# Extra expert blocks in pairs or one by one: the order of the blocks at the end of a mixture-of-experts loop

## The reference

```python
def hier_moe(h, rg_w, rg_b, re_w, re_b, w_gate, w_up, w_down):
    ...
    grp = jnp.argmax(g_logits, axis=-1)
    ...
    top_v, top_i = lax.top_k(e_sel, TOP_K_INNER)
    ...
    for g in range(N_GROUPS):
        hid = jax.nn.silu(jnp.einsum('td,edf->tef', t, w_gate[g])) * jnp.einsum('td,edf->tef', t, w_up[g])
        y = y + jnp.einsum('tef,efd->td', hid * combine[:, g, :, None], w_down[g])
```

## Time and profile before

| what | value |
|---|---|
| median of 3 runs | 718.06 us (713.32 to 723.28) |
| the profiled execution: its own time | 719.2 us |
| the profiled execution: span from first to last instruction | 717.4 us |
| mean granted clock of TensorE in it | 0.917 of full speed |
| PE busy | 585.8 us (82%) |
| DVE, ACT, POOL busy | 332.9, 143.7, 113.4 us |
| DMA moved | 180.99 MB, mean 252 GB/s |

### The profile page before, as it was taken

One profiled execution on the slowest core, in us unless ns is written; L12 is line 12 of the kernel. 1 busy time (PEld: TensorE's weight loads), 2 busy tenths in 40 slices (PEclk: granted clock), 3 DMA queues, 4 the chain that ended last, 5 costly groups with the idle time before them and its releaser, 6 DMA issues.

```text
span 717.4 us, 10963 instructions
## 1 busy us (share of the span) xinstructions
PE 585.8 (82%) x4542; PEld 366.9 (51%) x4542; DVE 332.9 (46%) x600; ACT 143.7 (20%) x371; POOL 113.4 (16%) x150
## 2 busy tenths in 40 slices
PE   3779999899987678999836999897877877769791
PEld 2459999676764365444524555443433444435320
DVE  2463442555642663496686244433333333343355
ACT  1441441254332153011111100000000000000132
POOL 4000000100001013000021232322222222221213
PEclk9769999999998599999965999999999999999887
DMA  8991311002006989901399799999999999998072
GB/s 302 370 248 60 69 62 56 16 1 91 27 1 220 375 306 273 311 30 60 109 407 364 288 413 410 411 409 408 409 413 411 410 408 406 408 401 313 31 266 117
DMA packets 71289, 180.99 MB, mean 252 GB/s; under 512 B 22164, under 2 KB 26108, under 8 KB 66628
## 3 DMA queue, kind: packets, MB, share of 16 engines
q1 hardware_dynamic: 60612, 163.39, 60.9%
q0 software_dynamic: 7936, 14.09, 5.6%
q10 hardware_dynamic: 2688, 2.77, 1.1%
HBM read 176.25 MB, written 14.45 MB: 266 GB/s over the span
## 4 chain that ended last, share of the span: by engine, by line
PE 44%; SPq 28%; DVE 11%; DMA 9%; ACT 4%; issue 3%; ACTq 0%; DVEq 0%; POOLq 0%
SPq L438 27%; PE bank L973 8%; PE bank L1219 8%; PE bank L1040 6%; PE bank L1323 5%; DMA ring<-in_ada_w_dram 3%; DMA ring<-in_moe_w_up_dram 3%; PE bank L1341 2%; PE bank L927 2%; PE bank L1022 2%; DMA x_tok<-in_x_sample_dram 2%; PE bank L1064 1%; PE bank L1081 1%; DVE x_tok L1912 1%; PE bank L1382 1%
## 5 line engine op out<-in xcount | busy, mean ns | idle before, releaser
L1323 PE MATMUL bank<-late_w,xT 128*64 128x256 f32 x672 | 83.4, 401 | 22.7 <-DMA late_w<-in_moe_w_up_dram 19.8
L1844 DVE COPY xT<-bank 128x512 f32<-128x512 f32 x38 | 26.2, 692 | 125.0 <-PE bank L1309 124.5
L1323 PE MATMUL bank<-ring,xT 128*64 128x256 f32 x480 | 64.8, 427 | 21.0 <-DMA ring<-in_moe_w_up_dram 19.0
L1323 PEld LDWEIGHTS bank<-late_w,xT 128*64 128x64 f32 x672 | 50.0, 139 | 62.2 <-DMA late_w<-in_moe_w_up_dram 30.5
L1323 PEld LDWEIGHTS bank<-ring,xT 128*64 128x64 f32 x480 | 37.4, 149 | 52.6 <-DMA ring<-in_moe_w_up_dram 28.5
L862 ACT ACTIVATE sgl<-bank 128x128 f32<-128x128 f32 x36 | 10.0, 278 | 249.3 <-PE bank L1323 249.3
L614 POOL DMA_INDIRECT expert_rows<-ye,dsti x36 | 36.6, 1016 | 128.2 <-DVE ye L1863 124.8
L607 POOL DMA_INDIRECT xg<-h_scratch,srci x38 | 39.0, 1026 | 102.6 <-PE bank L1309 92.7
L1860 DVE SCALAR_TENSOR_TENSOR S<-bank,modrt,S 128x512 f32<-128x512 f32 x36 | 27.0, 750 | 32.6 <-PE bank L1341 32.3
L1341 PE MATMUL bank<-late_w,hT 128*64 128x512 f32 x168 | 40.7, 604 | 0.0
L1040 PE MATMUL bank<-ring_r,h_high 128*128 128x512 f32 (+1 forms) x140 | 38.1, 412 | 0.0
(11 more groups left out here) (329 smaller groups left out, 858.1 us busy)
## 6 DMA issues: line engine op xcount, KB each, us to landing
ring<-in_ada_w_dram SPq DMA_DIRECT2D x22, 1024.0 KB, 11.3
late_w<-in_moe_w_gate_dram SPq DMA_DIRECT2D x21, 1024.0 KB, 16.9
late_w<-in_moe_w_up_dram SPq DMA_DIRECT2D x21, 1024.0 KB, 22.4
late_w<-in_moe_w_down_dram SPq DMA_DIRECT2D x21, 1024.0 KB, 22.4
ring<-in_moe_w_down_dram SPq DMA_DIRECT2D x15, 1024.0 KB, 22.7
ring<-in_moe_w_gate_dram SPq DMA_DIRECT2D x15, 1024.0 KB, 16.6
ring<-in_moe_w_up_dram SPq DMA_DIRECT2D x15, 1024.0 KB, 22.5
ring<-in_w_in_dram SPq DMA_DIRECT2D x7, 1024.0 KB, 5.6
```

The source lines that it names most:

```text
L1323: mm = pe.matmul(bank[2 + a][f * C:(f + 1) * C, 0:2 * P], x, w[:, kk, f, :, :], start=(kk == 0), stop=(kk == KD - 1))
L1844: dve.tensor_copy(xT[:, a, :, :], bank[a][:, :].rearrange("p (k n) -> p k n", k=4)).then_inc(xe_ev, 1)
```

## The change

It touches only the extra blocks and the last two steps of the static loop.

1. PE and DVE turn and copy the rows of blocks 32 and 33 inside the static loop, in the steps of experts 31 and 32 (the condition `e + 1 < E` goes). Before, both were turned behind the last `down` of the static loop, and copied behind its last `gated_rows`.
2. Inside a pair, PE, ACT, DVE and POOL finish the first block before they begin the second. Before, each kind of step was done for both blocks in turn.

```diff
@@ POOL
                         if b + 2 < NBLK:
                             pool.wait_ge(pe_xe, b + 1)
                             gather(b + 2, b % 2)
-                    for b in (E + 2 * i, E + 2 * i + 1):
                         scatter(b, b % 2)
@@ PE
-                if e + 1 < E:
-                    turn_x((e + 1) % 2, 16 * ((e + 1) // 2 + 1), e if e >= 1 else None)
+                turn_x((e + 1) % 2, 16 * ((e + 1) // 2 + 1), e if e >= 1 else None)
...
-            for b in (E, E + 1):
-                turn_x(b % 2, 16 * (b // 2 + 1), b - 1)
             pe.wait_ge(xe_ev, E + 2)
...
                         gate_up(b % 2, b % R, 32 * (b // R + 1), b + 1, b - 1)
-                    for b in (E + 2 * i, E + 2 * i + 1):
                         turn_h(b % 2, b + 1, b)
                         if b + 2 < NBLK:
                             turn_x(b % 2, 16 * ((b + 2) // 2 + 1), b + 1)
@@ DVE
-                if e + 1 < E:
-                    evac_x((e + 1) % 2, e + 2, gate_up_done(e - 1) if e >= 1 else None)
+                evac_x((e + 1) % 2, e + 2, gate_up_done(e - 1) if e >= 1 else None)
...
-            for b in (E, E + 1):
-                evac_x(b % 2, b + 1, gate_up_done(b - 2))
...
                         hidden(b % 2, b + 1, b - 1)
-                    for b in (E + 2 * i + 2, E + 2 * i + 3):
-                        if b < NBLK:
-                            evac_x(b % 2, b + 1, gate_up_done(b - 2))
-                    for b in (E + 2 * i, E + 2 * i + 1):
+                        if b + 2 < NBLK:
+                            evac_x(b % 2, b + 3, gate_up_done(b))
                         gated_rows(b, 16 * (b // 2))
```

## The result

The changed kernel took 733.95 us (median of 6 runs, 728.11 to 737.28) against 717.25 us for the kernel before (6 runs): a ratio of 1.0251, 95% interval 1.0212 to 1.0290, so 15 to 21 us slower. 733 was predicted, within 726 to 741.

The account below looks back on a forecast made before the run. Bound before: SP's weight loads, plus 10.7 us behind the last up matrix. Waits for gathers in the extra blocks add 14.8 us to the profiled 719.2, making 734.0; that profile lay 1.1 above the median, so 733 us, range 726 to 741.

Parts of the forecast that it names:

- The ring: Extra blocks: PE's turn waits for a gather queued behind the previous block's scatter; last `down` 14.8 us later; chance 0.70.
- The order itself: Rival theory of the experiments, no chance given: working extra blocks singly idles PE and lowers its clock, whatever POOL does.
- The link of 6.74 us: Extra blocks: from a turn's start through `down`, weighing and scatter to the next gather's start, without clock loss: 6.74 us.
- the quiet ones: Gathers of blocks 36 and 37, issued after the last weights: taken to land in 3.0 us each.
- The clock: Turns and `down`s behind PE's waits lose 1.6 us each in blocks 32 and 33, 0.8 each in 34 and 35.
- Two signs: Expected waits: PE's turns 2 to 3 us in blocks 34 and 35; POOL some 10 to 15 us for DVE.
- The seam: Static loop to extra blocks: `gate_up` of block 32 starts 3.4 us earlier, at about 641.4, but that is worth nothing.
- Quick gathers: Rival: every gather lands in 2.6 us, idling under 2 us, clock holds; last `down` 1.9 late, 720 us; chance 0.13.
- The gain: Rival: all four gathers land within 2.1 us; below that weights decide, 1.8 us gained, about 716 us; chance 0.05.
- Slow gathers to the end: Rival: gathers take 6.4 us in the quiet too, adding 6.8 us and 1.6 of clock: 741 us; chance 0.12.

Follow-up runs that it names:

- e1: Changed kernel with POOL's old order in a pair put back, both gathers and then both scatters: 725.66 us, ratio 1.0117 to the kernel before.
- e2: Changed kernel with the turn of block b + 2 moved behind `down` of block b, its copy behind the weighing: 724.49 us, ratio 1.0109.
- e5: Changed kernel with a pair's gathers ahead of its scatters and the next pair's turns and copies behind the second `gate_up`: 712.64 us, ratio 0.9984.
- e9: e5 measured again, unaltered: 712.16 us, ratio 0.9950 to the kernel before.
- e6: Changed kernel with unread matmuls ahead of the turn, six in blocks 32 and 33, one in later ones: 725.73 us, ratio 1.0193.
- e3: Changed kernel with turns and copies of blocks 32 and 33 put back behind the static loop, blocks still one by one: 730.60 us, ratio 1.0191.
- e4: Kernel before with only the turns and copies of blocks 32 and 33 moved into the static loop: 717.57 us, ratio 1.0006.
- e7: Changed kernel without gathers, turns and copies of blocks 36 and on, which hold no rows: 729.58 us, ratio 1.0225.

## Why the prediction was right

*The ring.* Shown: the four turns wait 5.28, 5.99, 1.06 and 1.81 us for their gathers, the chain runs over gather, `down`, weighing and scatter, and undoing either the order on POOL or the turn ahead of the `down` takes 10 or 11 us off the stretch (e1, e2); with both undone nothing of the loss is left (e5, e9). *The order itself* falls: e5 works the blocks one by one and is no slower than the kernel before.

*The terms.* The link of 6.74 us held: from the turn at 655.92 to the gather at 664.88 are 8.96 us, of which the slow clock took 2.2. The gathers landed in 6.55, 6.33, 2.15 and 2.15 us; I had 6.6, 6.1, 3.0 and 3.0, so the quiet ones were 1.7 us too long together, because I took a value between a gather beside the end of the weights (3.6) and a scatter in the quiet (2.6). The clock I had too cheap where the wait was long: turn and `down` took 4.7 us in blocks 32 and 33 (655.92 to 660.63, 671.25 to 676.02) instead of 2.5, so 2.2 each against my 1.6; 0.15 and 1.4 in blocks 34 and 35 against 0.8 each. The two misses nearly cancel, which is luck: 14.8 us predicted for the last `down`, 14.6 in the profile. Two signs came out smaller than forecast because the last gathers were quick: PE waited 1.06 and 1.81 us in blocks 34 and 35 instead of 2 to 3, and POOL 6.7 and 8.1 us ahead of their scatters instead of 10 to 15. The windows of 1 us of the changed kernel (length, busy share of PE with its matmuls, granted clock, DMA share, GB/s; the earlier trace rows has the same columns) show the clock falling while PE waits:

```profile
653.00:654.00 1.00, 0.00 (x0) 0.79 0.98 381
...
656.00:657.00 1.00, 1.00 (x6) 0.50 1.01 381
...
660.00:661.00 1.00, 1.00 (x8) 0.79 0.65 258
...
692.00:693.00 1.00, 1.00 (x6) 0.50 0.00 0
```

So all of the turn of block 34 and nearly all of the `down` of block 32 ran at 1.2 GHz, the granted clock of 0.50. In the kernel before, the clock fell only once the work had begun again at 644.82, in the window ahead of the earlier trace rows:

```profile
645.00:646.00 1.00, 1.00 (x10) 0.96 1.01 414
```

e6 shows that the lost clock was on the path.

*The seam.* `gate_up` of block 32 began 9.8 us behind that of block 31, as computed (641.4 against 631.7), and the 3.4 us were worth nothing (e3, e4).

*The rivals.* Quick gathers held for the two without rows and not for the two under the weights. But its premise that the clock holds while idling stays under 2 us did not come true: the turn behind the wait of 1.81 us, at 691.54, ran at the low clock too (1.13 us, the last window above). The gain needed 2.1 us for all four; only the last two came near it. Slow gathers to the end did not occur. The Trainium skill ("DMA: Bandwidth & Descriptors", section "Anatomy of one DMA — SWDGE (gpsimd) path") has a fixed part of about 2.0 us and adds the bytes: the gathers that move no rows, with the DMA engines quiet, agree with 2.15 us, while the ones beside the weights took 6.3 to 6.6. My 128 rows of 2 KB, 0.26 MB, were too many for these blocks: by the profile's DMA view of e7, the scatters of blocks 34 and 35 moved 0.11 and 0.16 MB, and with the DMA engines quiet they landed in 2.4 and 2.6 us. Gathers without rows, on the other hand, took 4.7 and 3.6 us beside the end of the weights. So as far as these rows show, what else was moving counted for more than the rows of a block.

*What the prediction had too simple.* It set the change against one profile of the kernel before, with the `gate_up` of block 35 at the low clock. The second profile shows that this comes and goes, for up to 3.4 us. The 733 us also stood on a median of 718.06 us for the kernel before, so they forecast 14.9 us more; by the medians it was 16.7 and 17.5. The forecast is closer to the time than to the difference, and that is luck as well. In the sums of the chances, 0.39 and 0.12 make 0.51 and not 0.52, and the low end of the ring against the median is 728 (718.06 + 14.8 - 5.2), not 726; neither changes the forecast.

## What to carry to other kernels

Where two buffers alternate and a later gather is issued on the same queue as the scatter of the block before, the order on that queue decides whether the gather is a prefetch or a link of the chain; look at the queue of the engine that issues it before the order on the engine that computes. A step that waits for a prefetch must not stand ahead of the step that the prefetch's own queue is waiting for. When a wait of several microseconds is added on PE, price the matmuls behind it at the lower clock as well.

## What the runs showed of the hardware that was not expected

Gathers with rows landed in 6.3 to 6.6 us beside the weights (at 380 to 420 GB/s, or in their tail, where the rate fell from 217 to 25), those without rows in 2.15 us with quiet DMA engines, alike in both profiles of the changed kernel (2.15 and 2.16). Scatters of 0.11 and 0.16 MB took 2.4 and 2.6 us in the same quiet (e7).

After a wait of over 5 us TensorE's granted clock was 0.50 when the turn began, and turn and `down` cost 4.7 us instead of 2.5; six matmuls that nobody reads were enough to keep it at 1.00. The length of the last wait alone does not tell: behind 1.81 us the clock was 0.50 (block 35 of the changed kernel), behind 1.94 us it was 1.00 (e5).

From the start of the last `down` to the first matmul behind the nested `If` blocks, PE took 4.2 to 4.6 us in ten of the twelve profiles. It took 8.67 us in e2, where PE waited for a copy first, and 6.70 us in e7, with a second packet on q8 in that time.
